# Next layer's variance through PSUM, three scalings behind the scaled tiles, more wide products at the norms

## What is computed

```
x_new = x + gt1 * rmsnorm(yx, g_post1[i])          # after the mixer ("post1")
hx2   = rmsnorm(x, g_pre2[i]) * (1.0 + sc2) + sh2   # input of the FFN ("pre2")
x     = x + gt2 * rmsnorm(swiglu(hx2, ...), g_post2[i])   # after the FFN ("post2")
# next layer begins with rmsnorm(x, g_pre1[i+1]) * (1 + sc1) + sh1   ("pre1")
def rmsnorm(x, g): return x * rsqrt(mean(x * x) + EPS) * g
```

## Time and profile before

| | |
|---|---|
| runs | 2146.09, 2147.15, 2147.22 us, median 2147.15 |
| the profiled execution | 2145.96 us, of which the span from first to last instruction is 2144.1 |
| PE, DVE, ACT, POOL busy | 2091.3 (98%), 1294.7 (60%), 810.2 (38%), 797.1 (37%) us |
| mean granted PE clock | 0.991 |
| boundary A | last mixer product starts 685.56, first FFN product 698.02 |
| boundary B | last FFN product starts 1260.25, first layer-1 product 1281.18, first query product 1302.83 |
| boundary C | last mixer product starts 1739.56, first FFN product 1751.94, second pair of FFN outputs 1766.88 |

### The profile page before, as it was taken

One profiled execution on the slowest core, in us unless ns is written; L12 is line 12 of the kernel. 1 busy time (PEld: TensorE's weight loads), 2 busy tenths in 40 slices (PEclk: granted clock), 3 DMA queues, 4 the chain that ended last, 5 costly groups with the idle time before them and its releaser, 6 DMA issues.

```text
span 2144.1 us, 27849 instructions
## 1 busy us (share of the span) xinstructions
PE 2091.3 (98%) x11142; PEld 1769.1 (83%) x11142; DVE 1294.7 (60%) x1779; ACT 810.2 (38%) x1263; POOL 797.1 (37%) x374
## 2 busy tenths in 40 slices
PE   9999999999999999999999999999999999999997
PEld 7788888888888888888888887888777878888885
DVE  8479899566864778767517775889745352111113
ACT  5479211334234422222212346862244452222123
POOL 3311333223344533333323365114344564444442
PEclk9999999999999999999999989999999999999998
DMA  7200212223452243533323313012233413323322
GB/s 280 64 17 23 61 55 62 81 80 108 152 192 79 70 129 130 193 97 126 106 79 117 95 62 108 22 45 93 69 104 92 139 59 108 99 89 98 96 81 69
DMA packets 74976, 205.28 MB, mean 96 GB/s; under 512 B 17888, under 2 KB 19168, under 8 KB 74848
## 3 DMA queue, kind: packets, MB, share of 16 engines
q1 hardware_dynamic: 70384, 194.22, 28.9%
q10 hardware_dynamic: 4464, 9.28, 1.2%
HBM read 197.79 MB, written 5.68 MB: 95 GB/s over the span
## 4 chain that ended last, share of the span: by engine, by line
PE 80%; DVE 11%; ACT 5%; issue 2%; DMA 2%; POOL 1%; ACTq 0%; SPq 0%; DVEq 0%; POOLq 0%
PE ps L610 72%; DVE conv_acc L1805 3%; DVE ps L1805 2%; PE ps L837 2%; ACT probs L1211 1%; PE ps L875 1%; DVE ada_raw L1618 1%; PE ps L855 1%; PE ps L699 1%; DMA w_raw<-in_w 1%; PE ps L690 1%; PE ps L720 1%; ACT pt1h L1239 1%; PE ps L638 1%; POOL w_l L497 1%
## 5 line engine op out<-in xcount | busy, mean ns | idle before, releaser
L497 POOL TENSOR_TENSOR w_l<-w_raw,w_h 128x1024 fp32r<-128x1024 f32 (+3 forms) x296 | 675.0, 2285 | 1049.3 <-ACT w_h L1013 1049.0
L610 PE MATMUL ps<-h_h,w_h 128*128 128x512 f32 (+1 forms) x1296 | 429.7, 372 | 9.6 <-ACT t L1305 4.2
L610 PE MATMUL ps<-h_h,w_l 128*128 128x512 f32 (+1 forms) x1296 | 423.4, 367 | 0.0
L610 PE MATMUL ps<-h_l,w_h 128*128 128x512 f32 (+1 forms) x1296 | 423.1, 366 | 0.0
L1013 ACT ACTIVATE w_h<-w_raw 128x1024 fp32r<-128x1024 f32 (+3 forms) x296 | 277.2, 938 | 222.1 <-PE ps L610 133.7
L610 PEld LDWEIGHTS ps<-h_h,w_h 128*128 128x128 f32 x1296 | 242.9, 188 | 59.8 <-ACT t L1305 6.0
L610 PEld LDWEIGHTS ps<-h_l,w_h 128*128 128x128 f32 x1296 | 243.7, 188 | 44.1 <-issue 1.2
L610 PEld LDWEIGHTS ps<-h_h,w_l 128*128 128x128 f32 x1296 | 243.5, 188 | 43.1
L1618 DVE CUSTOM_DVE_ANT_0 ps<-ada_raw,c_row 128x1024 f32<-128x1024 f32 x160 | 270.1, 1688 | 9.6 <-DMA ada_raw<-in_ada 4.5
L610 PE MATMUL ps<-f_h,w_h 128*128 128x258 f32 (+1 forms) x672 | 173.1, 339 | 1.2 <-DVE t L1993 1.2
L610 PE MATMUL ps<-f_h,w_l 128*128 128x258 f32 (+1 forms) x672 | 173.5, 340 | 0.0
(11 more groups left out here) (253 smaller groups left out, 3117.3 us busy)
## 6 DMA issues: line engine op xcount, KB each, us to landing
w_raw<-in_w SPq DMA_DIRECT2D x216, 512.0 KB, 3.6
ada_raw<-in_ada SPq DMA_DIRECT2D x80, 512.0 KB, 3.7
w_raw<-in_w SPq DMA_DIRECT2D x56, 256.0 KB, 3.2
w_raw<-in_w SPq DMA_DIRECT2D x16, 384.0 KB, 3.1
ada_near<-in_ada SPq DMA_DIRECT2D x10, 512.0 KB, 10.1
ada_far<-in_ada SPq DMA_DIRECT2D x6, 512.0 KB, 15.3
x_again<-in_x ACTq DMA_DIRECT2D x8, 384.0 KB, 7.6
x_between<-x SPq DMA_DIRECT2D x8, 384.0 KB, 2.6
```

The lines of the kernel that those rows point to most:

```text
L497: nc.gpsimd.tensor_tensor(wl[:, s % RING, 0:n], raw[:, s % RAW, 0:n], wh[:, s % RING, 0:n], ALU.subtract).then_inc(split, 1)
L610: ins = nc.tensor.matmul(at(out, c0, c1), w[:, s % RING, b * P:(b + 1) * P], m[:, kt, first + c0:first + c1], start=(kt == 0 and n == 0), ...
```

## The change

At A, B and C, PE gets two groups of two wide products more: one after the first spread, ahead of the wait for the last addition to `xgy_sum`, and one between the sums of `xgy` and `gsq`. In B the first two groups grow from 3, 3 to 5, 4. In `next_variance` the two intermediate values lie in PSUM columns instead of in `x_sq`, and a seventh instruction copies the new sum of squares back to `x_sq`, which before was updated in place. In B and C the scalings of tiles 5, 6, 7 move from behind `next_variance` to behind the scaled tiles 0, 1 and 2. In B, POOL waits for the last addition to `xgy_sum` before it splits the last slab that it has to split ahead of the x additions.

```
@@ gpsimd, layer 0, after the x_times of post2
+                    pool.wait_ge(*seen("vadd", 0, "post2", KT - 1))
                     split_run(at_s, SLABS + RING)
@@ tensor, renorm
                 spread(lo, st, ly, st, to=factor(ly, st))
                 if nxt:
+                    keep_warm(s, 2)
                     pe.wait_ge(*seen("vadd", ly, st, KT - 1))
                     token_sums(xgy_sum, lo, "xgy", stop=False)
+                    keep_warm(s, 2)
                     pe.wait_ge(*seen("uadd", ly, st, KT - 1))
@@ tensor, post2
-                renorm(ly, "post2", lo, (1, "pre1") if ly == 0 else None, SLABS, (3, 3, 6))
+                renorm(ly, "post2", lo, (1, "pre1") if ly == 0 else None, SLABS, (5, 4, 6))
@@ vector, next_variance
+                change, total = DD[:, 64:64 + n], DD[:, 96:96 + n]
-                link(v.scalar_tensor_tensor(out=new, in0=token_sum("xgy", ...), scalar=2.0, in1=new,
+                link(v.scalar_tensor_tensor(out=change, in0=token_sum("xgy", ...), scalar=2.0, in1=new,
-                link(v.tensor_tensor(new, new, r, ALU.mult), dve_tmp)
-                link(v.tensor_tensor(old, old, new, ALU.add), dve_tmp)
+                link(v.tensor_tensor(change, change, r, ALU.mult), dve_tmp)
+                link(v.tensor_tensor(total, old, change, ALU.add), dve_tmp)
-                link(v.tensor_scalar(buf, old, 1.0 / D, EPS, ALU.mult, ALU.add), dve_tmp)
+                link(v.tensor_scalar(buf, total, 1.0 / D, EPS, ALU.mult, ALU.add), dve_tmp)
+                v.tensor_copy(old, total).then_inc(*dve_tmp.up())
                 link(v.reciprocal(buf, buf), dve_tmp, "var", *nxt)
@@ vector, renorm
                 next_variance(ly, st, lo, nxt)
-                for k in pool_adds[1:]:
-                    post_scale(ly, st, lo, k)
                 dve.wait_ge(*seen("spread", *nxt))
                 for k in K_ORDER[1]:
                     if k in (1, 2, 3):
                         residual(k)
                     scaled(k)
+                    if k < 3:
+                        post_scale(ly, st, lo, k + 5)
```

More of the change, by code:

```diff
@@ L1512, in next_variance @@
                 link(v.tensor_tensor(new, token_sum("gsq", TOK["gsq"] + t0, n), r, ALU.mult), dve_tmp)
-                link(v.scalar_tensor_tensor(out=new, in0=token_sum("xgy", TOK["xgy"] + t0, n), scalar=2.0, in1=new,
+                change, total = DD[:, 64:64 + n], DD[:, 96:96 + n]
+                link(v.scalar_tensor_tensor(out=change, in0=token_sum("xgy", TOK["xgy"] + t0, n), scalar=2.0, in1=new,
                                             op0=ALU.mult, op1=ALU.add), dve_tmp)
-                link(v.tensor_tensor(new, new, r, ALU.mult), dve_tmp)
-                link(v.tensor_tensor(old, old, new, ALU.add), dve_tmp)
+                link(v.tensor_tensor(change, change, r, ALU.mult), dve_tmp)
+                link(v.tensor_tensor(total, old, change, ALU.add), dve_tmp)
                 buf = token_rs[:, TOK[nxt[1]] + t0:TOK[nxt[1]] + TT]
-                link(v.tensor_scalar(buf, old, 1.0 / D, EPS, ALU.mult, ALU.add), dve_tmp)
+                link(v.tensor_scalar(buf, total, 1.0 / D, EPS, ALU.mult, ALU.add), dve_tmp)
+                v.tensor_copy(old, total).then_inc(*dve_tmp.up())
                 link(v.reciprocal(buf, buf), dve_tmp, "var", *nxt)
```

## The result

The changed kernel takes 2156.76 us (median of 4 runs, 2154.58 to 2159.67) against 2146.78 us (4 runs, 2146.09 to 2147.22): a ratio of 1.0044, 95% interval 1.0031 to 1.0057, so slower by 0.4%. The profiled execution is the longest of the four, 2159.67 us; that of before took 2145.96.

What follows compares the result with a forecast made beforehand. PE, busy for 98% of the span, bounds the kernel, so only its waits and unread work matter; -2.0 (A) + 3.5 (B) + 6.9 (C) = +8.4 on 2145.96, median 1.2 above: told as 2155.5 us, range 2150.5 to 2162.5.

Steps and rivals of the forecast that it cites:

- A: Boundary ahead of FFN products: wide products and variance through PSUM were to save time, -2.0 us.
- B: Boundary ahead of the first layer-1 products: -4.4 up to the first scaled tile, +7.9 behind it, +3.5 us in all.
- C: Boundary with the same loop as B at 512 columns: late lows and half clock, +6.9 us, between +4.5 and +9.
- The moved scalings: B and C: late scalings delay POOL's additions and the eight lows behind them; +7.0 and +5.3 us before clock loss.
- The half clock behind the wait: B and C: after idling, PE runs 5 us at half clock, losing 2.3 us in B and 2.2 in C.
- The rival in which the clock returns at once: Lows bind, but full clock returns at once or never falls: +5.5 us, 2152.7; chance 0.16.
- Clock held in B's sums: B up to the first scaled tile: sums at full clock and POOL's later split bring it 4.4 us earlier.
- The end that the prediction kept for a fallen clock: B up to the first scaled tile: if the clock falls in the sums, only -1.5 us.
- the other end: A if the clock falls all the same: PE starts 0.9 later, only the wait goes, -0.4 us.
- The reciprocal: A: it stays in SBUF, now beside a POOL instruction; taken as 0.2 us, not waiting for POOL.
- the first of the bounds: A: the reciprocal's time was bounded by 0.2 and 1.2 us; the first was taken.
- an estimate of 1 us lost: By the skill's PSUM cost rule, five DVE instructions at each of three boundaries give 1 us back; rows disagreed.

Runs made afterwards that it cites:

- e1: The changed kernel with the scalings of tiles 5, 6, 7 put back ahead of the scaled tiles; 2142.66 us, ratio 0.9982 to the original kernel.
- e2: The original kernel with only the scalings of tiles 5, 6, 7 moved behind scaled tiles; 2164.2 us, ratio 1.0077.
- e3: The changed kernel with POOL's additions of tiles 4 to 7 and its lows interleaved in B and C; 2145.63 us, ratio 0.9998.
- e4: The changed kernel with 24 more wide products, read by nobody, during PE's wait for the lows in C; 2154.9 us, ratio 1.0039.
- e6: The original kernel with the new wide products alone; 2146.10 us, ratio 0.9997.
- e8: e1 with tile 7's scaling behind scaled tile 0, new wide-product groups of 3 in B, none in C; 2143.01 us, ratio 0.9985 to the original kernel.
- e7: The original kernel with only POOL's slab split in B waiting for the last addition; 2147.33 us, ratio 1.0013.
- e5: The original kernel with only the variance's intermediate values in PSUM columns; 2146.26 us, ratio 0.9998.

## Why the prediction was right, and where it wasn't

The forecast was 2155.5 and slower; the median is 2156.76, inside the range, and e1, e2 and e3 show that the mechanism is the one named. That the two numbers lie within 1.3 us of each other is in part luck: the four runs lie 5 us apart, and in the profiled one the boundaries came to +11.6, not +8.4, with B's sums out by 3.0.

- **The moved scalings** were the step that decided, and its sizes held. First low behind the first scaled tile: 13.8 forecast, 13.74 measured in B; 9.4 and 9.53 in C. Lows end: 28.6 and 28.18 in B, 19.7 and 19.49 in C. What made the forecast right is that the three additions and the eight lows were followed as one queue.
- **The half clock behind the wait** was taken as 5 us of products; it was 4.2 us in B and 5.6 us in C, the rest of each stretch of 10.2 us lying in the wait. The price held too: 2.2 forecast in C, 2.5 by e4. e4 also shows it in B, where the clock fell sooner in the wait, 2.9 us of products ran at half clock, and the part behind the first scaled tile was 0.6 us shorter (32.02 against 32.65). The rival in which the clock returns at once fell.
- **Clock held in B's sums**, the term of -4.4, failed in the profiled execution: the first scaled tile came only 1.4 us earlier, with two stretches at half clock still there. The price of the term is right where the clock does hold and all parts are in, as in e4 (-4.2; e1, with the scalings ahead of the tile, -3.6). e6, whose clock held until the sums had ended, has the wide products alone and -2.0. But of the five executions with these groups of 5, 4, 2 and 2 (after, e1, e3, e4, e6) the clock held up to the first scaled tile in two. The end that the prediction kept for a fallen clock, -1.5, is what the profile of after has. B is +7.1 there, not +3.5: 3.0 of the 3.6 us missed are this term, the rest is the part behind the first scaled tile, +8.6 and not +7.9. PE's last low step ended there 31.9 us behind the tile, as forecast (32.0); but then PE waited 0.78 us for a copy by DVE (L1717), a wait that the forecast didn't have.
- **A** was taken as -2.0 and is -2.5; e1 and e8 agree (31.37, 31.39). Where the clock fell, as in e3 and e4, the same instructions end at 34.50 and 34.33, so the other end was not -0.4 but about +0.5.
- **C** was +6.9 and is +7.0, from two small errors that cancel: the first scaled tile came 0.6 earlier, not 0.2, and the part behind it was +7.6, not +7.1.
- **The reciprocal** beside POOL took 0.18 us (A, above), which settles the first of the bounds for it. The Trainium skill, SBUF — State Buffer, "Who interferes with whom", leaves a reciprocal out of the instructions that POOL locks out; this trace agrees. The Trainium skill's other rule, a fixed cost of 120 cycles from PSUM to SBUF against 58 from SBUF to SBUF (VectorE: DVE Perf Modes, "The TRN2 errata"), led to an estimate of 1 us lost. The row at L1522 above, from PSUM to SBUF, takes 0.16 us, and the one without PSUM in the earlier trace rows 0.17, so nothing of it shows here.
- **Left out**: the 2 us away from the boundaries, the sum of +2.1, +1.8 and -1.9. Nothing of the change touches those places. The clock fell at 382 to 384 us in six of the ten profiled executions, e2 and e7 among them and before, e1, e5 and e6 not, and at 1450 us in that of after alone.

## What to carry to other kernels

A step that looks free on its own engine can be the head of another engine's queue: before moving it, write down everything that stands in order behind the instruction that uses its result, and not that instruction alone. If the step must be late, split that queue by due time (e3 took back 7.6 of 8.6 us in B with no change on DVE). Wide products against a falling clock are a chance and not a switch; judge them by the clock in several executions, since one trace can show either case.

## What the runs showed of the hardware that was not expected

The granted clock falls at different places in executions of kernels that run the same instructions there: eight wide products in A took 2.09 us in after and 3.63 in e6; the stretches at 0.50 ahead of the last boundary were 3.4, 6.8, 10.2 or 13.7 us long. It goes with a spread of the runs of one kernel of 13 to 17 us (before 2142.7 to 2155.8, e1 2136.6 to 2153.9), more than the change itself is worth without the moved scalings. In e1 the fastest run had a mean granted clock of 0.996 and the slowest one of 0.989.

The five long waits for the lows (B and C in after and in e2, B in e4) each have a stretch at 0.50 of 10.2 us. In after it began 3.3 us (B) and 2.0 us (C) into the wait and outlasted it by 4.2 and 5.6 us, though products were being issued again. In C of e4, 24 wide products inside the wait, the last ending 1.1 us before the next real one, were enough to keep it up.
